# Feed-forward way in as seven products of halves, with the weight remainders split three to VectorE and four to GpSimd

## The reference

```
D_MODEL = 1024; D_FF = 2816
def swiglu(h, w_in, w_out):                    # h: tokens x 1024, w_in: 1024 x 5632
    gate, up = jnp.split(h @ w_in, 2, axis=-1)
    return (jax.nn.silu(gate) * up) @ w_out    # w_out: 2816 x 1024
x = x + mx[5] * swiglu(modulate(rms_norm(x, norm2_g[i]), mx[3], mx[4]), ffn_w_in[i], ffn_w_out[i])
if need_ctx_out:                               # layer 0 only: the 256 context tokens too
    y_ctx = y_ctx + mc[5] * swiglu(modulate(rms_norm(y_ctx, norm2_g[i]), mc[3], mc[4]), ...)
```

## Time and profile before

| | |
|---|---|
| runs | 3026.23, 3027.04, 3032.28 us (median 3027.04) |
| span of the profiled execution | 3029.1 us |
| busy PE / DVE / ACT / POOL | 95% / 48% / 40% / 44% |
| ff0, PE from its first to its last matmul | 438.95 to 995.9 us |
| ff1, PE from its first to its last matmul | 1553.83 to 1917.5 us |

### The profile page before, as it was taken

The page is one execution under the profiler, slowest core; times in us unless marked ns, Lnnn a source line. Parts: engine busy times, 40 slices in busy tenths (PEclk is TensorE's granted clock), DMA queues, the critical chain, the costliest instruction groups (busy, mean ns, idle before and its releaser), DMA issues.

```text
span 3029.1 us, 41310 instructions
## 1 busy us (share of the span) xinstructions
PE 2864.1 (95%) x15994; PEld 2151.8 (71%) x15994; DVE 1450.7 (48%) x2336; ACT 1221.4 (40%) x1993; POOL 1332.4 (44%) x770
## 2 busy tenths in 40 slices
PE   7999989999999899999999999998888989989997
PEld 4878768888888789898878888783663348556533
DVE  3556656532321734334441112656565656557665
ACT  5666542111112533333342222436335653454464
POOL 3665425444533435444355555477440027763100
PEclk9999999999999999999999999999999979999999
DMA  6102314433321112112133332220358843124694
GB/s 248 43 22 83 141 74 155 149 144 134 126 76 62 57 49 77 63 56 76 44 122 98 98 97 91 70 84 21 113 209 334 343 144 98 42 65 187 268 398 188
DMA packets 85968, 374.88 MB, mean 124 GB/s; under 512 B 9424, under 2 KB 11984, under 8 KB 76688
## 3 DMA queue, kind: packets, MB, share of 16 engines
q1 hardware_dynamic: 68640, 311.75, 28.9%
q10 hardware_dynamic: 12528, 43.73, 3.7%
q0 software_dynamic: 4608, 16.78, 1.5%
HBM read 556.77 MB, written 29.36 MB: 194 GB/s over the span
## 4 chain that ended last, share of the span: by engine, by line
PE 81%; DVE 7%; DMA 3%; POOL 3%; ACT 3%; issue 2%; SPq 0%; DVEq 0%; POOLq 0%; ACTq 0%
PE PS L106 79%; PE PS L109 2%; DMA ALL<-in_moe 2%; DVE SCR L121 1%; DMA BF<-in_ada 1%; POOL RTX L121 1%; DVE XF L127 1%; DVE SM L121 1%; ACT SCR L115 1%; DVE RTX L118 1%; POOL XF L124 1%; ACT RT L115 1%; POOL RT L121 1%; POOL WL L121 0%; DVE SCR L127 0%
## 5 line engine op out<-in xcount | busy, mean ns | idle before, releaser
L106 PE MATMUL PS<-RT,WH 128*128 128x512 f32 (+1 forms) x5632 | 1508.6, 368 | 40.6 <-DVE RT L127 9.1
L106 PEld LDWEIGHTS PS<-RT,WH 128*128 128x128 f32 x5632 | 1010.9, 190 | 263.0 <-issue 30.8
L121 POOL TENSOR_TENSOR WL<-RAW,WH 128x1024 fp32r<-128x1024 f32 x284 | 704.9, 2484 | 716.9 <-ACT WH L115 716.9
L106 PE MATMUL PS<-RT,WL 128*128 128x512 f32 (+1 forms) x2816 | 927.2, 365 | 0.0
L115 ACT ACTIVATE WH<-RAW 128x1024 fp32r<-128x1024 f32 x284 | 299.0, 1056 | 592.1 <-PE PS L106 531.9
L106 PEld LDWEIGHTS PS<-RT,WL 128*128 128x128 f32 x2816 | 491.4, 190 | 59.6
L121 POOL TENSOR_TENSOR RT<-SCR,RT 128x512 fp32r<-128x512 f32 (+2 forms) x146 | 197.9, 1364 | 324.5 <-ACT RT L115 231.9
L106 PE MATMUL PS<-RTX,SCR 128*32 128x512 f32 x1176 | 286.3, 621 | 7.3 <-DMA RTX<-placed_out,PLACE 7.3
L106 PE MATMUL PS<-ALL,SCR 128*32 x576 | 268.8, 611 | 24.0 <-DVE SCR L121 14.3
L121 DVE TENSOR_TENSOR SCR<-PS,SCR 128x512 f32<-128x512 f32 (+1 forms) x106 | 58.9, 572 | 469.8 <-PE PS L106 455.2
L127 DVE SCALAR_TENSOR_TENSOR XF<-PS,SM,XF 128x512 f32<-128x512 f32 x240 | 151.1, 658 | 244.3 <-PE PS L106 244.0
(11 more groups left out here) (272 smaller groups left out, 3750.1 us busy)
## 6 DMA issues: line engine op xcount, KB each, us to landing
...
RAW<-in_ff SPq DMA_DIRECT2D x132, 512.0 KB, 3.6
BF<-in_ada SPq DMA_DIRECT2D x64, 512.0 KB, 4.7
RAW<-in_ret SPq DMA_DIRECT2D x64, 512.0 KB, 3.3
RTX<-in_ada SPq DMA_DIRECT2D x30, 512.0 KB, 7.0
RAW<-in_win SPq DMA_DIRECT2D x28, 512.0 KB, 3.4
XF<-placed_in ACTq DMA_DIRECT2D x24, 512.0 KB, 8.7
```

Source lines behind the costliest of these rows:

```text
L106: return NOTHING if self.e is None else self.e.matmul(o, w, x, start=first, stop=last)
L121: return NOTHING if self.e is None else self.e.tensor_tensor(*a)
```

## The change

The first hidden tile of each stage stays plain (`pe_ff_first`). Each of the other 21 is a 2x2 by 2x2 block product: the two halves of K (four blocks each) against gate and up for the weights, and against the two halves of the tokens for `h` (B11, B12, B21, B22; 384 tokens a half in ff0, 256 in ff1). It is done in seven products in place of eight (`GROUP`): seven weight pieces of 128x512, three of them halves as they are (q = 0, 4, 6) and four of them sums or differences of halves (q = 1, 2, 3, 5), against B11, B21, B22 and four sums T1 to T4 of the B. Each piece is four blocks by three matmuls of 384 or 256 columns, 84 matmuls a tile.

What else goes with it: DVE makes the four weight sums and the low parts of q = 0, 4, 6, POOL the low parts of the sums; ACT makes seven high parts of 128x512. The partial results are put together by three copies on ACT (a, q, p), three adds out of PSUM and two multiplications on DVE, two adds on POOL, and accumulation onto the open PSUM banks. T1 to T4 (four K blocks each) are made in the norm by DVE, their high parts by ACT, their low parts by DVE (T3, T4) and POOL (T1, T2). Weights are loaded and kept as half units (256 KB, six slots, refilled piece by piece); the products of ada1 are spread one to a group (two in the first three) and one to an output tile; CHUNKS becomes (4, 4, 4, 4, 4, 2).

```diff
-CHUNKS = (4, 4, 4, 4, 3, 3)
+CHUNKS = (4, 4, 4, 4, 4, 2)
...
+GROUP = (("a", "B11", True), ("q", "T3", True), ("p", "T1", True), ("r", "T2", True), ("q", "T4", False),
+         ("p", "B22", False), ("a", "B21", False))
...
+        def low_engine(s, n):
+            kind, i, q = PIECES[n]
+            return dve_done if kind == "mix" and q in {"ff0": (0, 4, 6), "ff1": (0, 4, 6)}[s] else pool_done
...
+        def piece_high(act, s, n):
+            hi, lo = piece(s, n)
+            wait_slot(act, s, n)
+            held = raw_of_piece(s, n)
+            if held:
+                wait_half(act, s, *held)
+                act.activation(hi, raw_half(s, *held), ACT.Copy).then_inc(*act_done.done(("phi", s, n)))
+            else:
+                act.wait_ge(*dve_done.at(("sum", s, n)))
+                act.activation(hi, piece_sum(s, n), ACT.Copy).then_inc(*act_done.done(("phi", s, n)))
...
+        def piece_low(eng, done, s, n):
...
+            eng.wait_ge(*act_done.at(("phi", s, n)))
+            if sum_over(n):
+                eng.wait_ge(*dve_done.at(("sum", s, sum_over(n))))
+            x = raw_half(s, *held) if held else piece_sum(s, n)
...
+            eng.tensor_tensor(lo, x, hi.bitcast(F32), ALU.subtract).then_inc(*done.done(*events))
...
+        def piece_add(dve, s, n):
+            kind, i, q = PIECES[n]
+            o = piece_sum(s, n)
+            wait_slot(dve, s, n)
+            if q == 1:
+                wait_half(dve, s, i, 0)
+                wait_half(dve, s, i + 1, 0)
+                dve.tensor_tensor(o, raw_half(s, i, 0), raw_half(s, i + 1, 0), ALU.subtract).then_inc(*dve_done.done(("sum", s, n)))
+            elif q == 2:
+                wait_half(dve, s, i + 1, 1)
+                dve.tensor_tensor(o, raw_half(s, i + 1, 0), raw_half(s, i + 1, 1), ALU.add).then_inc(*dve_done.done(("sum", s, n)))
+            elif q == 3:
+                dve.wait_ge(*dve_done.at(("sum", s, n - 1)))
+                dve.tensor_tensor(o, piece_sum(s, n - 1), raw_half(s, i, 0), ALU.subtract).then_inc(*dve_done.done(("sum", s, n)))
+            else:
+                wait_half(dve, s, i, 1)
+                dve.wait_ge(*dve_done.at(("sum", s, n - 2)))
+                dve.tensor_tensor(o, raw_half(s, i, 1), piece_sum(s, n - 2), ALU.subtract).then_inc(*dve_done.done(("sum", s, n)))
...
+        SUMS = (("T1", ("B12", "B11")), ("T3", ("B22", "B12")), ("T2", ("B22", "T1")), ("T4", ("B21", "T2")))
+        T_ORDER = ("T3", "T1", "T2", "T4")
+        T_LOW = {"T3": "dve", "T4": "dve", "T1": "pool", "T2": "pool"}
...
+        def ff_norm_dve(dve, s, parts, A, before):
...
+            for k in K_ORDER:
+                for j, _, n in parts:
+                    dve.wait_ge(*pe_done.at(("rb", s, j)))
+                    dve.scalar_tensor_tensor(normed(s, k)[:, :, part_of_half(j)], in_halves(XS[j][:, k, :]),
+                                             A[:, 8 * j + k:8 * j + k + 1], in_halves(bank.of(("rb", s, j))[:, 0:n]),
+                                             ALU.mult, ALU.mult).then_inc(*dve_done.done(("h", s, k, j)))
...
+                if k >= 4:
+                    ff_norm_low(dve, dve_done, s, k - 4, parts)
+            for kk in range(4):
+                dve.wait_ge(*act_done.at(("hb", s, kk + 4)))
+                for x, (a, b) in SUMS:
+                    if x in ("T2", "T4"):
+                        dve.wait_ge(*dve_done.at((b, s, kk)))
+                    dve.tensor_tensor(plain_operand(s, x, kk, 1), normed_half(s, a, kk), normed_half(s, b, kk), ALU.subtract
+                                      ).then_inc(*dve_done.done((x, s, kk)))
+            for x in ("T3", "T4"):
+                for kk in range(4):
+                    t_low(dve, dve_done, s, x, kk)
...
+        def ff_norm_pool(pool, s, parts, before):
...
+            for kk in range(4):
+                ff_norm_low(pool, pool_done, s, kk + 4, parts)
+            for x in ("T1", "T2"):
+                for kk in range(4):
+                    t_low(pool, pool_done, s, x, kk)
...
+        def pe_ff_group(pe, s, c, f):
+            fi = hidden_tile(c, f)
+            for q, (name, x, opens) in enumerate(GROUP):
+                n = mix_at(c, f, q)
+                wait_piece(pe, s, n)
+                if opens:
+                    o = take_bank(pe, (s, name, fi), HALF[s])
+                else:
+                    o = bank.of((s, name, fi))[:, 0:HALF[s]]
+                    pe.wait_ge(*act_done.at((s, "copy", name, fi)))
+                for kk in range(4):
+                    if fi == 1 and x[0] == "T":
+                        pe.wait_ge(*act_done.at((x, s, kk)))
+                        pe.wait_ge(*(dve_done if T_LOW[x] == "dve" else pool_done).at(("tlo", x, s, kk)))
+                    w = [y[:, P * kk:P * kk + P] for y in piece(s, n)]
+                    events = [("pc", s, n)] if kk == 3 else ()
+                    if opens:
+                        three(pe, o, w, operand_pair(s, x, kk), kk == 0, kk == 3, events)
+                    else:
+                        three_onto(pe, o, w, operand_pair(s, x, kk), events)
...
+                    for q, name in enumerate(("a", "q", "p")):
+                        n = mix_at(c, f, q)
+                        act.wait_ge(*pe_done.at(("pc", s, n)))
...
+                        elif name == "a":
+                            act.wait_ge(*dve_done.at((s, "G2", fi - 1)))
+                            act.wait_ge(*pool_done.at((s, "u2", fi - 1)))
+                        elif name == "q":
+                            act.wait_ge(*dve_done.at((s, "act", fi - 1)))
+                        else:
+                            act.wait_ge(*pool_done.at((s, "s75", fi - 1)))
+                        act.activation(COPY[name][:, 0:nh], bank.of((s, name, fi))[:, 0:nh], ACT.Copy).then_inc(
+                            *act_done.done((s, "copy", name, fi)))
+                        if q == 0 and f:
+                            act_tile_high(act, s, c, f - 1, parts)
+                        hi_upto(act, ("pc", s, n))
...
+                if _c or _f:
+                    ADA1_AT["group", _c, _f] = 2 if (_c, _f) in ((0, 1), (0, 2), (0, 3)) else 1
+            if _c < len(CHUNKS) - 1:
...
-                    for j, _, n in parts:
-                        v = act_ring.of((s, c, f, j))[:, 0:n]
-                        dve.wait_ge(*act_done.at((s, "silu", c, f, j)))
-                        dve.wait_ge(*pe_done.at((s, "up", c, f, j)))
-                        dve.tensor_tensor(v, bank.of((s, "up", c, f, j))[:, 0:n], v, ALU.mult).then_inc(
-                            *dve_done.done((s, "act", c, f, j)))
-                        bank.give((s, "up", c, f, j), dve_done.now())
...
+                    for q in range(2):
+                        sum_upto(dve, s, ("pc", s, mix_at(c, f, q)))
+                    dve_ada1_at(dve, s, "group", c, f)
+                    sum_upto(dve, s, ("pc", s, mix_at(c, f, 2)))
+                    dve.wait_ge(*pe_done.at(("pc", s, mix_at(c, f, 3))))
+                    dve.wait_ge(*act_done.at((s, "copy", "a", fi)))
+                    u2 = COPY["a"][:, 0:nh]
+                    dve.tensor_tensor(u2, bank.of((s, "r", fi))[:, 0:nh], u2, ALU.add).then_inc(*dve_done.done((s, "U2", fi)))
+                    bank.give((s, "r", fi), dve_done.now())
+                    sum_upto(dve, s, ("pc", s, mix_at(c, f, 3)))
+                    dve.wait_ge(*dve_done.now())
...
+                    dve.tensor_tensor(UP[:, 0:nh], bank.of((s, "q", fi))[:, 0:nh], u2, ALU.add).then_inc(
+                        *dve_done.done((s, "u1", fi)))
...
+                    sum_upto(dve, s, ("pc", s, mix_at(c, f, 4)))
+                    dve.wait_ge(*pe_done.at(("pc", s, mix_at(c, f, 5))))
+                    if fi >= 2:
...
+                    dve.tensor_tensor(v2, bank.of((s, "p", fi))[:, 0:nh], u2, ALU.add).then_inc(*dve_done.done((s, "G2", fi)))
...
+                    sum_upto(dve, s, ("pc", s, mix_at(c, f, 5)))
+                    sum_upto(dve, s, ("pc", s, mix_at(c, f, 6)))
+                    dve.wait_ge(*pool_done.at((s, "u2", fi)))
+                    dve.wait_ge(*act_done.at((s, "silu", fi, 1)))
+                    dve.tensor_tensor(v2, v2, COPY["q"][:, 0:nh], ALU.mult).then_inc(*dve_done.done())
+                    dve.wait_ge(*act_done.at((s, "silu", fi, 0)))
+                    dve.wait_ge(*dve_done.at((s, "u1", fi)))
+                    dve.tensor_tensor(v1, v1, UP[:, 0:nh], ALU.mult).then_inc(*dve_done.done((s, "act", fi)))
...
+                    lo_upto(pool, ("pc", s, mix_at(c, f, 0)))
+                    if f:
+                        pool_tile_low(pool, s, c, f - 1, parts)
+                    lo_upto(pool, ("pc", s, mix_at(c, f, 1)))
+                    s7, s5, u2 = (COPY[x][:, 0:nh] for x in ("q", "p", "a"))
+                    pool.wait_ge(*act_done.at((s, "copy", "p", fi)))
```

(63 more changed lines are left out.)

456 lines of the change are left out of this document (377 added, 79 removed).

## The result

The change made the kernel slower: 3082.86 us (3079.83 to 3086.58) against 3029.66, a ratio of 1.0175 (1.0160 to 1.0189), some 53 us. The forecast was 3017, ten less than before.

A forecast was written before the change was run, and what follows sets the result against it. PE, busy 95% of the span, was taken as the bound. 3029.1 - 63 saved + 28.3 for the starts + 20 stall in ff1 + 5 in ff0 = 3019.4 us of span, 2.1 less for the median: 3017 us, range 2990 to 3048.

The forecast's parts named there:

- What PE saves: PE's matmuls in ff0 and ff1: seven products in place of eight save 46 and 17.5 us, 63 us in sum.
- The start: Ahead of each stage's second tile PE waits for DVE and POOL: 17 us lost in ff0, 11.3 in ff1.
- cold start of 1.3: PE after an idle gap: lower granted clock, first six matmuls 1.3 us slower.
- What a tile asks of DVE and POOL: Shared DVE and POOL work plus idle time per tile: 12.0 us in ff1 against PE's 10.0, 14.3 in ff0 against 14.6.
- look-ahead: Six slots in ff1: pieces made ahead during a way out are worth 4.6 us, so a four-tile chunk stalls 3.4.
- The stall at the end of a chunk: Last chunk of ff1, two tiles: its last hidden tile comes late behind only two blocks of matmuls; 2.5 us.
- what costs nothing: Half transfers, the attention constants' load, ACT's copies and silus: all hidden, no time added.
- Half transfers come late: Rival on weight loading: two raw units hold one tile, so halves load late; 0.4 us a tile, 3034 us, chance 0.03.
- DVE and POOL bound both stages: Rival: DVE's line of waits idles 1.4 us a tile in ff0 and ff1; slower, 3038 to 3051 us, chance 0.20.
- No overlap at all: Rival: DVE and POOL each stand for the other's whole instruction, their times add up; 3090 us, chance 0.04.
- the two cases: Rivals setting the range: slots hide ff1's stalls, early starts (2987, chance 0.23); DVE and POOL bound both stages, late starts (3051, 0.20).

The follow-up runs named there:

- ff1_plain: The changed ff0 kept, all of ff1 with its code and chunks of before; 3010.65 us, ratio 0.9941 to the kernel before.
- five_on_dve: The changed kernel with five of seven low parts on DVE in ff1 and two on POOL; 3084.54 us, ratio 1.0196.
- sum_first: `hidden_first` with DVE in ff1 making the sum for product 5 ahead of the low part of product 4; 3055.46 us, ratio 1.0092.
- port_load: `hidden_first` plus one DVE sum of 512 per ff1 tile, both inputs in SBUF, in DVE's idle time; 3049.04 us, ratio 1.0068.
- line_load: `hidden_first` plus one DVE memset of 128x512 per ff1 tile, reading nothing, in DVE's idle time; 3048.20 us, ratio 1.0065.
- hidden_first: The changed kernel; in ff1 ACT and POOL serve a chunk's last hidden tile ahead of way-out pieces in slots freed by products 3 to 6; 3045.07 us, ratio 1.0052.

## Why the prediction was wrong

**What PE saves** was right: tiles of 14.60 us in ff0 (14.6) and 10.07 in ff1 (10.0), matmuls of 384 and 256 columns as bounded (14.60 / 84 = 0.174 and 10.07 / 84 = 0.120 us).

**The start** was nearly right. In ff0 the forecast had the second tile begin 35.6 us after the first scaling (436.45 to 472.1); DVE and PE after:

```profile
470.75 3.55 DVE L148 TENSOR_TENSOR BFR<-BF,BFR 128x384 fp32r<-128x384 f32 x4
474.22 0.68 DVE L148 TENSOR_TENSOR WL<-RAW,WH 128x512 fp32r<-128x512 f32 x1
...
475.04 0.98 PE L130 MATMUL PS<-RT,WH 128*128 128x384 f32 x2 [13.17 <-DVE WL L148]
```

It is 36.6 (scaling from 438.47). PE stood idle 13.2 us ahead of it, forecast 16, and 8.8 in ff1, forecast 10. In ff1 26.2 us (1537.67 to 1563.87) for 25.2; the tile behind it takes 13.2, 3.1 over its 10.07, where a cold start of 1.3 had been put. ff0 lost some 6 us more than forecast in its first chunk (tiles of 17.3, 15.9 and 15.7, a way out of 38.2 for 33.7) and in its last: of 24 us forecast it kept 17.5 (`ff1_plain`).

**What a tile asks of DVE and POOL** gave the right number by a reason that does not hold, which is luck. The tiles that stall take 12.0 us, as forecast; the sum of shared work is not what sets them, since with less of it (`five_on_dve`) they took 13.3, and DVE is busy 17.4 and POOL 18.6 of 24.3 us. Nor is the order alone (`sum_first`). What is shown is that DVE and POOL beside each other lengthen the tile (`port_load` against `line_load`). That a chain goes round DVE, ACT and POOL once a tile, with links lengthened in this way, is how I read the timelines; no run cuts it, and which link could be cut with profit stays open. The look-ahead was sized well: 3.9 us a chunk lost (11.92 + 12.10 - 2 x 10.07) against 3.4.

**The stall at the end of a chunk** is the step that failed. The forecast charged the late hidden tile once, 2.5 us, in the last chunk of ff1, "only two blocks of three matmuls" ahead of it. Each of the other way outs has six blocks, 4.1 us, ahead of its last hidden tile, and it was taken for granted that the tile's silu, product, high and low part follow at once. They do not: they stand in line, on ACT behind high parts whose transfers wait for the tile's own last low part, on POOL behind four low parts. The five way outs took 142.8 us for 5 x 21.7 and the last 20.3 for 10.9: 44 us in place of 2.5. Added to the forecast, this alone turns its sign. `hidden_first` gives 30 us of ff1 back by order alone (426.4 to 396.1; 38 between the medians), which shows the cause; half of what stays, 7 us, is the last chunk's. But `hidden_first` is still 17 us slower than before, with some 13 us of such waits left in it: even with this step put right altogether, by this estimate, the change would have come out near no gain. The half transfers, put among what costs nothing since a whole one lands in 3.6 us, stand first in the timeline of the wait: each of the two raw units is free only when its low part is made. But they begin no sooner in `hidden_first`; what costs is to stand in line behind them. No run changes the transfers themselves.

Each such wait is also paid twice: PE starts again slowly.

```profile
1684.08 0.63 PE L130 MATMUL PS<-RT,WL 128*128 128x512 f32 x1
1684.51 1.06 PE L130 MATMUL PS<-RT,WH 128*128 128x512 f32 x2
...
1687.36 0.40 PE L130 MATMUL PS<-RT,WL 128*128 128x512 f32 x1
```

A single matmul is shown with 0.63 and a little later with 0.40 us; 28.3 - 21.7 - 4.63 leaves 2 us for it, with the granted clock at 0.94 over that window (1.00 in the way out of `hidden_first`).

Of the **rivals** none was this. "Half transfers come late" named the first link and priced it over all tiles; "DVE and POOL bound both stages" had the sign, and the line of waits, but in the tile. "No overlap at all" came nearest in time, 3090 us, by a mechanism that did not occur: it asked tiles of 14.3 us in ff1 and 17.1 in ff0, and they took 12.0 and 14.60. (The stated range, 2990 to 3048, ends 3 us inside the ends of the two cases that it is taken from, 2987 and 3051; with 3083 us measured that changes nothing.)
